# Mixers: memory probabilities turned beside the stick-breaking scores, multiplied beside the fox scores, copied ahead of a split and the logarithm

## The reference

```python
u = _rmsnorm(h, mix_pre_g[l])
proj = u @ w_in[l]
q_sb, k_sb, v_sb, q_fx, k_fx, v_fx, f_logit, q_mem = jnp.split(proj, split_at, axis=-1)
o_sb = _stick_breaking_attention(...)   # log_sigmoid(z), reversed cumulative sum, exp
o_fx = _forgetting_attention(...)       # softmax(z + c_q - c_k), causal
# memory attention: 256 memory tokens, no mask
z = jnp.einsum('bhqd,bhkd->bhqk', q, k).astype(jnp.float32) * (q.shape[-1] ** -0.5)
p = jax.nn.softmax(z, axis=-1)
o_mem = jnp.einsum('bhqk,bhkd->bhqd', p.astype(v.dtype), v)
g_sb, g_fx, g_mem = jnp.split(jax.nn.sigmoid(u @ w_gate[l] + b_gate[l]), N_BRANCH, axis=-1)
merged = g_sb * (o_sb @ w_br_sb[l]) + g_fx * (o_fx @ w_br_fox[l]) + g_mem * (o_mem @ w_br_mem[l])
h = h + _rmsnorm(merged @ w_out[l], mix_post_g[l])
```

## Time and profile before

| | |
|---|---|
| median of 3 runs | 1848.41 us (1848.38 to 1849.37) |
| the profiled execution | 1848.37 us |
| its span, first to last instruction | 1846.6 us |
| granted TensorE clock | 1.00 |
| busy: TensorE, VectorE, ScalarE, GpSimd | 99%, 70%, 59%, 11% |
| chain that ended last | TensorE 95%, VectorE 2%, ScalarE 1%, DMA 1% |
| DMA | 333.94 MB, mean 181 GB/s |

### The profile page before, as it was taken

One profiled execution on the slowest core, in us unless ns is written; L12 is line 12 of the kernel. 1 busy time (PEld: TensorE's weight loads), 2 busy tenths in 40 slices (PEclk: granted clock), 3 DMA queues, 4 the chain that ended last, 5 costly groups with the idle time before them and its releaser, 6 DMA issues.

```text
span 1846.6 us, 28820 instructions
## 1 busy us (share of the span) xinstructions
PE 1829.8 (99%) x10951; PEld 1633.7 (88%) x10951; DVE 1287.2 (70%) x2040; ACT 1090.1 (59%) x1884; POOL 205.9 (11%) x158
## 2 busy tenths in 40 slices
PE   8999999999999999999999999999999999999998
PEld 7888899998888888888999888888889998889997
DVE  6775747787777567755777778755768765768863
ACT  7665545556666466645555657655557655757653
POOL 0220001110022002200011102210002210001210
PEclk9999999999999999999999999999999999999999
DMA  9765575455576558655654548654747664536753
GB/s 269 208 188 183 168 198 171 140 156 177 171 225 192 189 150 232 186 192 141 191 179 141 188 146 230 190 194 145 220 139 217 190 198 152 176 103 198 204 192 103
DMA packets 435721, 333.94 MB, mean 181 GB/s; under 512 B 25338, under 2 KB 381312, under 8 KB 435584
## 3 DMA queue, kind: packets, MB, share of 16 engines
q1 hardware_dynamic: 435008, 331.57, 59.8%
q10 hardware_dynamic: 576, 0.53, 0.1%
HBM read 330.97 MB, written 1.05 MB: 180 GB/s over the span
## 4 chain that ended last, share of the span: by engine, by line
PE 95%; DVE 2%; ACT 1%; DMA 1%; issue 0%; ACTq 0%; SPq 0%
PE bank L1751 16%; PE bank L1728 14%; PE bank L1730 14%; PE bank L1729 14%; PE bank L1739 7%; PE bank L1741 7%; PE bank L1740 7%; PE bank L1753 7%; PE bank L1757 2%; PE bank L1750 1%; DVE wlo L1103 1%; DVE U L1156 1%; PE bank L2003 0%; PE bank L2069 0%; PE bank L2074 0%
## 5 line engine op out<-in xcount | busy, mean ns | idle before, releaser
L1103 DVE TENSOR_TENSOR wlo<-raw,whi 128x1024 fp32r<-128x1024 f32 (+3 forms) x638 | 761.7, 1201 | 289.6 <-ACT whi L578 280.2
L578 ACT ACTIVATE whi<-raw 128x1024 fp32r<-128x1024 f32 (+3 forms) x638 | 647.0, 1023 | 330.4 <-PE bank L1730 244.8
L1751 PE MATMUL bank<-U,whi 128*128 128x512 f32 x1280 | 438.4, 395 | 0.2 <-DVE wlo L1103 0.2
L1753 PE MATMUL bank<-U,wlo 128*128 128x256 f32 x1120 | 314.6, 281 | 0.0
L1739 PE MATMUL bank<-U,whi 128*128 128x256 f32 x1024 | 289.2, 282 | 0.0
L1741 PE MATMUL bank<-U,wlo 128*128 128x256 f32 x1024 | 286.3, 280 | 0.0
L1740 PE MATMUL bank<-U,whi 128*128 128x256 f32 x1024 | 285.7, 279 | 0.0
L1751 PEld LDWEIGHTS bank<-U,whi 128*128 128x128 f32 x1280 | 229.9, 188 | 42.9 <-DVE wlo L1103 0.7
L1728 PE MATMUL bank<-whi,U 128*128 128x384 f32 (+2 forms) x592 | 219.3, 370 | 2.8 <-DVE U L1156 2.0
L1728 PE MATMUL bank<-whi,hhi 128*128 128x512 f32 x560 | 219.3, 392 | 0.0
L1730 PE MATMUL bank<-wlo,hhi 128*128 128x512 f32 x560 | 218.1, 389 | 0.0
(11 more groups left out here) (307 smaller groups left out, 2365.1 us busy)
## 6 DMA issues: line engine op xcount, KB each, us to landing
raw<-in_ffn_w_up SPq DMA_DIRECT2D x351, 256.0 KB, 3.5
raw<-in_ffn_w_down SPq DMA_DIRECT2D x264, 256.0 KB, 2.9
raw<-in_ffn_w_gate SPq DMA_DIRECT2D x175, 256.0 KB, 3.4
raw<-in_w_gate SPq DMA_DIRECT2D x128, 192.0 KB, 3.0
raw<-in_w_in SPq DMA_DIRECT2D x80, 256.0 KB, 3.5
raw<-in_a_w_in SPq DMA_DIRECT2D x48, 256.0 KB, 3.3
raw<-in_w_mem_kv SPq DMA_DIRECT2D x32, 256.0 KB, 3.3
raw<-in_w_out SPq DMA_DIRECT2D x32, 256.0 KB, 3.0
```

Source lines behind the costliest of these rows:

```text
L578: act.activation(whi[n % SLOTS][:, 0:w], raw[n % RAW][:, 0:w], ACT.Copy).then_inc(hi_ready, 1)
L1103: dve.tensor_tensor(wlo[n % SLOTS][:, 0:w], raw[n % RAW][:, 0:w], whi[n % SLOTS][:, 0:w].bitcast(F32), ALU.subtract).then_inc(lo_ready, 1)
L1751: ins = pe.matmul(dst, wh, u2[:, k, :], start=(k == 0), stop=(k == KT - 1))
L1753: pe.matmul(dst[:, 0:TOK], wl, uhi[:, k, :], start=False, stop=False)
```

## The change

Three things are written in another order in each of the eight pairs; no instruction is added or removed. On TensorE the four transposes of the memory probabilities move from behind feature chunk 3 to ahead of it, right behind the SB scores, and the memory product moves from behind gate chunk (0, 1) to ahead of it, right behind the fox scores. On ScalarE the copy of the transposed probabilities (`mem_pT`) moves from behind the logarithm to ahead of the split that stands before the logarithm. Their waits move with them.

```diff
@@ ScalarE
                     act.activation(sb_e[:, :, :], sb_e[:, :, :], ACT.Exp, scale=-1.0).then_inc(sb_act, 1)
+                    act.wait_ge(mem_tp, I + 1)
+                    act.activation(mem_pT[:, :], bank[7][:, :], ACT.Copy).then_inc(mem_pt, 1)
                     split_to(c + 2 + SLOTS)
                     act.wait_ge(sb_act, I * 4 + 3)
                     act.activation(sb_e[:, :, :], sb_e[:, :, :], ACT.Ln, bias=1.0).then_inc(sb_act, 1)
-                    act.wait_ge(mem_tp, I + 1)
-                    act.activation(mem_pT[:, :], bank[7][:, :], ACT.Copy).then_inc(mem_pt, 1)
                     split_to(c + 4 + SLOTS)
@@ TensorE
                     ins.then_inc(sbz_full, 1)
-                    feature_chunk(3)
                     pe.wait_ge(mem_norm, I + 1)
                     for q in range(TT):
                         for k in range(TT):
                             ins = turn(mem_p[:, q * TOK + k * P:q * TOK + (k + 1) * P],
                                        bank[7][:, k * TOK + q * P:k * TOK + (q + 1) * P])
                     ins.then_inc(mem_tp, 1)
+                    feature_chunk(3)
                     gate_chunk(0, 0)
@@ TensorE
                     ins.then_inc(fxz_full, 1)
-                    gate_chunk(0, 1)
                     pe.wait_ge(mem_pt, I + 1)
                     for k in range(TT):
                         ins = pe.matmul(bank[6][:, 0:TOK], vmem[l][:, k, p * P:(p + 1) * P], mem_pT[:, k * TOK:(k + 1) * TOK],
                                         start=(k == 0), stop=(k == TT - 1))
                     ins.then_inc(o_full[MEM], 1)
+                    gate_chunk(0, 1)
                     gate_chunk(0, 2)
```

## The result

| | before | changed |
|---|---|---|
| median | 1848.9 us (1848.16 to 1850.31, 22 runs) | 1852.07 us (1850.68 to 1853.0, 22 runs) |
| the profiled execution | 1848.37 us, span 1846.6 | 1851.26 us, span 1849.5 |

The ratio is 1.0016, with a 95% interval of 1.001 to 1.0023: 3.0 us slower, between 1.8 and 4.3 (the two medians are 3.2 us apart). Forecast were 3.1 us, and 1851.5 us for the median. The measured median is 0.6 us above that; 0.5 of it is the kernel before, whose median was taken again beside the changed kernel and is that much above the one shown ahead.

A forecast was written before the change was run, and what follows sets the result against it. TensorE, 99% busy, bounds the kernel and already waits slightly for VectorE's run to the gates. Eight pairs by 0.39 us give 3.1 us on 1848.37: 1851.5 us; likeliest case 1850.8 to 1852.1, full range 1849.4 to 1853.0.

The forecast's parts named there:

- Transposes ahead of the chunk: TensorE, ahead of feature chunk 3: four transposes cost 0.44 us less 0.05 saved, so chunk and `kx` come 0.39 us later.
- The saving behind the 64-row matmuls: TensorE, behind the SB scores: an exposed weight load costs less before transposes; 0.05 us taken, bounds 0 and 0.11.
- The run on VectorE shifts whole: VectorE, from `kx` to the first gates: everything moves 0.39 us later, nothing gives way, `wlo` stays held by GpSimd.
- The first rival: VectorE: `wlo` runs before GpSimd's `sb_lo`, gates come early, only the wait at gate chunk (0, 0) is paid; chance 0.08.
- The waits don't add up: TensorE at gate chunks (0, 0) and (1, 0): the later clock, VectorE's, counts; 0.39 us a pair in all.
- The rival in which they add: VectorE waits for TensorE at the fox addition: 0.58 us a pair, 4.6 us slower, 1853.0 us; chance 0.12.
- neither wait matters: VectorE's run has unseen slack, TensorE keeps only its savings: about 1 us faster, 1847.5 us; chance 0.05.
- The division between the two waits: TensorE: new wait of 0.24 us at gate chunk (0, 0), wait at (1, 0) grows by 0.20.
- VectorE's clock: VectorE's run from `kx` to the gates sets when TensorE passes gate chunk (1, 0): 0.39 us later a pair.
- Product and copy: Memory product beside the fox scores, and `mem_pT` copy ahead of split and logarithm: cost 0, the logarithm covered by 1.4 us.
- The first rival's price: `wlo` in 0.96 instead of 2.51 us, gates about 1.5 us early; 0.12 us a pair, 1.0 us, 1849.4 us.

The follow-up runs named there:

- the bank 6 edit: Changed kernel, but feature chunk 3 goes to bank 6 and `kx` is made from there; 1852.15 us against 1848.96 before, ratio 1.0017.
- the larger dose: Kernel before with only the `mem_pT` copy moved ahead of split and logarithm, transposes left behind feature chunk 3; 1856.75 us against 1849.24, ratio 1.004.
- that run: Changed kernel with VectorE's split behind the fox maximum, held by GpSimd, done only behind `take_gate(p, 0)`; 1849.35 us against 1848.96, ratio 1.0001.

## Why the prediction was right

**Transposes ahead of the chunk.** Right in kind and size: `kx` was forecast 0.39 us later; it stands 4.39 us behind the SB scores' first matmul instead of 4.00, within 0.01 in all eight pairs. The saving behind the 64-row matmuls is there as taken from the latent attention. The rows of the changed kernel, TensorE:

```profile
328.97 0.40 PE L2053 MATMUL bank<-qs,ks 64*128 64x128 f32 x4
329.29 0.66 PE L1757 MATMUL bank<-cst,mem_p 128*128 128x128 f32 x4
329.70 0.36 PE L1739 MATMUL bank<-U,whi 128*128 128x256 f32 x1
329.91 0.28 PE L1740 MATMUL bank<-U,whi 128*128 128x256 f32 x1
```

Four transposes in 0.66 us instead of 0.60 means that the first truly began 0.06 after its load. The load is exposed here too. The Trainium skill's page "TensorE: Matmul & The Clock Gate" (section "Part 2: What happens when you issue a matmul") says that weight loads are pulled ahead of running matmuls where the row groups don't conflict or the load goes to the background buffer; the 0.06 us show that this didn't cover this load.

**The run on VectorE shifts whole.** Right: 10.98 against 10.97 us, the held `wlo` 2.51 as before, no idle mark in it. (Six of the run's twelve rows stand in rows 2, not seven.) The first rival (the order of `wlo` and `sb_lo` changes) didn't come.

**The waits don't add up.** Right, and shown by the bank 6 edit and by the larger dose. Over the same distance as above, from the SB scores to gate chunk (1, 0), TensorE needed 15.98 us a pair before, 16.37 in the changed kernel and 16.36 with the first wait taken away; with only the copy moved 16.88. The 0.39 a pair of the changed kernel are the forecast's, and eight times that is 3.1. The rival in which they add, 4.6 us, would give 1.0025, just outside the interval of the result (1.0023); that neither wait matters is far outside.

**The division between the two waits** was off: forecast were 0.24 us at gate chunk (0, 0) and 0.20 more at (1, 0) (0.56 from start to start), found 0.16 and 0.32 (0.68). I had taken the release of the load as 0.1 us behind VectorE, as at the gates; behind `kx` it was 0.05 (TensorE's next weight load starts at 333.73, `kx` ends at 333.68). That accounts for the first number and for 0.08 of the 0.12 in the second; the remaining 0.04, by which TensorE came to gate chunk (1, 0) sooner still, stay open. It changes nothing in the sum, because the sum was that of VectorE's clock: that part came out right although its two terms were mis-sized.

**Product and copy** at nothing: shown for the product by its own run's trace. For the copy it is shown only together with the transposes: the logarithm started at 332.29 and ended 1.6 us before VectorE used it at 334.70. The copy without the transposes cost 7.5 us, so its cover was the early transposes.

**The first rival's price** was argued wrong: without the held split VectorE is not 1.55 us earlier but 0.73, since ScalarE's exponentials come next; the expectation of that run already has it so. It would have changed nothing in that rival's time.

## What to carry to other kernels

Where a busy engine waits twice for the same helper within one run of the helper's work, price the change by the helper's clock: what moves the start of its run, and how long the run is. A wait that is taken away ahead of the last one comes back there; a step put ahead of the chunk that starts the run costs its length (here 0.44 us less a saving of 0.05) even if the busy engine does no more work. If a helper's step is held by another engine anyway, put the step that needs no such hold in front of it; before a step is moved later, look which buffers it gives back.

## What was not expected of the hardware

TensorE's weight load started 0.05 us behind the end of VectorE's `kx`, and 0.11 us behind the first half of the gates, in the same trace (that half lasts 0.61 us, so it ends at 344.41; the load starts at 344.52). In TensorE's program two waits stand ahead of the second load (for the gates, and for the weight chunk) and one ahead of the first; whether that is the cause wasn't tried.
